# One decay matrix for both scan directions: the time step moves into the exponent

## The chip, the cores and the metric

The kernel runs on one core of a Trainium2 chip. The metric is device time in microseconds (us) of one execution. The engines that matter here are TensorE (PE, matrix products), VectorE (DVE, elementwise work), ScalarE (ACT, activation functions and copies), GpSimd (POOL) and SyncE (SP, which issues the weight loads). Each engine works through its own list of instructions in order and waits on semaphores for the others.

## What is computed

The reference is one inference step of a two-layer trunk (D = 1024) over 384 tokens: 256 latent tokens and 128 context tokens. Each layer has one input projection, three token mixers beside each other (pooling, differential attention, and a bidirectional state-space scan called SSD), gates, branch and output projections, and a gated feed-forward block. The change touches the SSD scan alone:

```
xdt = x * dt
y_diag = einsum(cc, bc, exp(segsum(dt * a)), xdt)        # inside a chunk of 128 tokens
y_off  = einsum(cc, h_enter, exp(cumsum(dt * a)))        # from the state that enters the chunk
...
y = y_forward + flip(y_backward) + D * x                 # both directions, summed
```

There are 8 heads of 64 channels, in 2 groups of 4 heads that share the matrices B and C, and 3 chunks of 128 tokens (two latent, one context). For one head and one chunk, the inner part of a direction is a 128x128 matrix, decay(s, t) * dt(s) * (B C)(s, t), times the 128x64 block of x. The forward matrix is zero on one side of the diagonal, the backward one on the other; the diagonal belongs to both.

## The kernel before

One core computes everything, channels on the 128 partitions and the 384 tokens in the free dimension. Weights stream from memory in *units* of 128x1024 elements, and the order of the units (UNITS) is the order of all the work: per layer 8 units for the scan's inputs, then u, q, k, v, then 4 units z, 24 gate units, 12 branch units, 8 output units and the feed-forward block. For each unit SP loads it, ACT copies its high part (`hi`, L1155), DVE subtracts to get the low part (`lo`, L1508), and PE does three products for each of 8 blocks (`three`, L823 to L825: 128x128 weights on 384 columns). Three units of high and low parts are held at once, so ACT and DVE prepare unit u+3 while PE is at unit u.

The three token mixers have no weights of their own to stream. They are laid by hand into *slots*: slot s runs beside unit MIX0+s, MIX0 being the first z unit. On PE the mixers' part of a slot stands after the unit's products (function `mixers`). On DVE it stands in two parts around the preparation of the next weights (`mixers_a`, then `lo`, then `mixers_b`). Attention fills slots 0 to 14; the time steps dt are made in slots 1 to 3 (tiles dtv, dte, dtt, adt), and their running sums (tile sm) in slot 3. Then come the chunks' transposes (slots 14 to 16), the normalisation of the attention output (slots 15 to 19: rst, then ot) and the states between chunks (slots 16 to 20: xw, hst).

The scan itself is six tasks y_ = 0 to 5 (chunk c = y_ // 2, head group g = y_ % 2), one in every second slot from slot 19. A task goes round through three engines:

1. PE `rows` (L1053) spreads the running sums of 4 heads over 128 partitions, one bank for each direction.
2. DVE `decays` (L1782) adds to each head's 128x128 block a number per partition (tile nac, minus the running sum) and a mask of 0 and -1e30: 8 instructions, into tile ee, [direction][head x 128].
3. ACT exponentiates ee in place (L1397, 128x1024), and for the latent chunks also the banks into eb (L1396).
4. DVE `matrices` (L1793, L1797) multiplies each head's block of ee by dt (tile dtt, a number per partition) and by the group's B C matrix (tile bg): 8 instructions of 128x128. For the latent chunks it also multiplies eb by C, 128x512 for each direction. The last one raises m_done.
5. PE `scan_out` (L1075) waits for m_done and multiplies, two slots after `rows`: for each head two products of xt with ee (one for each direction) and, for the latent chunks, two of the entering states hst with eb, all into one 64x128 output. Even heads write partitions 0 to 63 and odd heads 64 to 127.
6. DVE `gate_z` (L1810, L1814) adds D x and multiplies by z. Then the next task's `decays` follows on DVE.

After the last task come the grouped normalisation (L1115, L1116, L1908), the split of its result into high and low parts, and the branch units of the scan.

`chunk_weights` (L1864, slot 7) also makes nac. `step.then(...)` raises a semaphore and makes the same engine wait for it, so that the next instruction may read the result.

Of the kernel before, what the change touches and what calls it, by code (L numbers as in the profile page):

```python
# [26 lines left out]
ALU = mybir.AluOpType  # L27
ACT = mybir.ActivationFunctionType
AX = mybir.AxisListType

P = 128
# [9 lines left out]
CHUNK0 = (0, P, CTX0)  # L41
NCH = 3
# [3 lines left out]
SSD_H, SSD_P, SSD_G = 8, 64, 2  # L46
# [4 lines left out]
FFN = ((8 * D // 3 + 127) // 128) * 128  # L51
FT = FFN // P
NEG = -1e30


XBC, UU, QQ, KK, VV, ZZ, GATE, BRANCH, OUT, UP, DOWN = (
# [165 lines left out]
def count(l, per, i):  # L222

    return l * per + i + 1
# [60 lines left out]
def build(nc, wstream, whead, par, bias, tab, xs, xp, cvec, cvec_rows, kc, vc, st0, fng, y, newk, newv, news):  # L285
    ctx = ExitStack()
    with ctx:
# [3 lines left out]
        def sem(name):  # L291
            return ctx.enter_context(nc.semaphore(name))
# [10 lines left out]
        with ExitStack() as a:  # L303
            gates = sb("gates", [P, 24, T], where=a)
            xbc = sb("xbc", [P, 8, T], where=a)
# [27 lines left out]
        with ExitStack() as a:  # L333
            xt = sb("xt", [P, NCH, 4 * P], where=a)
            bg = sb("bg", [P, NCH, 4 * P], where=a)
# [4 lines left out]
            ee = sb("ee", [P, 2, 4 * P], where=a)  # L340
            eb = sb("eb", [P, 2, 4 * P], where=a)
# [42 lines left out]
        dte = sb("dte", [P, 48])  # L384
        dtt = sb("dtt", [P, 48])
# [3 lines left out]
        sm = sb("sm", [P, 144])  # L389
# [97 lines left out]
        dt_in = sem("dt_in")  # L487
        dt_raw = sem("dt_raw")
        dt_log = sem("dt_log")
        adt_done = sem("adt_done")  # L490
        ada_done = sem("ada_done")
        bd_done = sem("bd_done")
# [270 lines left out]
        def _(pe):  # L763
# [293 lines left out]
            def scan_out(l, y_):  # L1057
                c, g = divmod(y_, 2)
                pe.wait_ge(m_done, count(l, NY, y_))
                if y_:  # L1060
                    pe.wait_ge(yz_done, count(l, NY, y_ - 1))
                else:
                    pe.wait_ge(st_done, count(l, 4, 3))
                    pe.wait_ge(state_in, 32 * (l + 1))
                for i in range(4):
                    h = 4 * g + i
                    out = mix7[64 * (i % 2):64 * (i % 2) + 64, P * (i // 2):P * (i // 2) + P]
                    hs = slice(SSD_P * h, SSD_P * h + SSD_P)
                    ms = slice(P * i, P * i + P)
                    terms = [(xt[:, c, hs], ee[:, d, ms]) for d in range(2)]  # L1070
                    if c < 2:

                        terms += [(hst[:, (0, 3)[d] if c == 0 else (2, 1)[d], hs], eb[:, d, ms]) for d in range(2)]
                    for n, (s_, m_) in enumerate(terms):
                        last = mm(out, s_, m_, start=(n == 0), stop=(n == len(terms) - 1))  # L1075
                last.then_inc(y_done, 1)
# [66 lines left out]
        def _(act):  # L1143
# [184 lines left out]
            def mixers(l, s):  # L1328
# [40 lines left out]
                if SLOT_A <= s < SLOT_A + HEADS:  # L1369
                    h = s - SLOT_A  # L1370
                    if h == HEADS - 1:
                        act.preload_act_table_set(LN_EXP)
                    act.wait_ge(misc_done, count(l, NMISC, M_ATT + h))
                    af(rst[:, h, :], mz, ACT.Copy).then_inc(att_ss, 1)
                    if h == HEADS - 1:
                        act.wait_ge(att_ss, count(l, HEADS, h))
                        step.then(af(rst[:, :, :], rst[:, :, :], ACT.Ln, bias=eps, scale=1.0 / P))
                        af(rst[:, :, :], rst[:, :, :], ACT.Exp, scale=-0.5).then_inc(ors_done, 1)
# [119 lines left out]
        def _(dve):  # L1498
# [287 lines left out]
            def matrices(l, y_):  # L1786
                c, g = divmod(y_, 2)
                dve.wait_ge(e_done, count(l, NY, y_))
                for d in range(2):
                    for i in range(4):  # L1790
                        col = 16 * c + SSD_H * d + 4 * g + i
                        m_ = ee[:, d, P * i:P * i + P]
                        last = stt(out=m_, in0=m_, scalar=dtt[:, col:col + 1], in1=bg[:, c, P * (2 + g):P * (3 + g)],  # L1793
                                   op0=ALU.mult, op1=ALU.mult)
                    if c < 2:
                        e3 = eb[:, d, :].rearrange("p (i t) -> p i t", i=4)
                        last = tt(e3, e3, xbc[:, 6 + g, CHUNK0[c]:CHUNK0[c] + P].unsqueeze(1).to_broadcast([P, 4, P]),  # L1797
                                  ALU.mult)
                last.then_inc(m_done, 1)

            def gate_z(l, y_):
# [16 lines left out]
            def mixers_a(l, s):  # L1818
                if s < NATT:
                    softmax_max(l, s)  # L1820
                if s == 1:
                    dve.wait_ge(misc_done, count(l, NMISC, M_DTT))
                    step.then(tt(dtv[:, :].rearrange("p (c h) -> p c h", c=NCH),
                                 mz[:, 0:48].rearrange("p (c h) -> p c h", c=NCH),
                                 prm_("dtb", 0, 16).unsqueeze(1).to_broadcast([P, NCH, 16]), ALU.add))
                    stt(out=dte[:, :], in0=dtv[:, :], scalar=-1.0, in1=dtv[:, :], op0=ALU.mult, op1=ALU.min) \
                        .then_inc(dt_raw, 1)
                if s == 3:
                    dve.wait_ge(misc_done, count(l, NMISC, M_SM))
                    nc.vector.tensor_copy(sm[:, :], mz[:, 0:144])  # L1830
                    step.then(nc.vector.tensor_copy(csh_[0:96, :], mz[0:96, 2 * P:3 * P]))
                    tt(csl[0:96, :], mz[0:96, 2 * P:3 * P], csh_[0:96, :].bitcast(F32), ALU.subtract).then_inc(sm_done, 1)
                if SLOT_PW <= s < SLOT_PW + 4:
                    j = s - SLOT_PW
                    dve.wait_ge(misc_done, count(l, NMISC, M_PW + j))
                    ts(ut[:, j, 0:T], mz, prm_("pscale", j), None, ALU.mult).then_inc(op_done, 1)
                if s == SLOT_SPLIT:
                    for i in range(4):
                        low(l, SP_OP + i, hl[:, i, :], ut[:, i, 0:T], hh[:, i, :])
                if scan_task(s, Y_SLOTS) is not None:  # L1840
                    gate_z(l, scan_task(s, Y_SLOTS))
                if SLOT_S <= s < SLOT_S + 2:
                    enter_state(l, s - SLOT_S)
                if SLOT_S - 1 <= s < SLOT_S + 3:
                    weighted(l, s - SLOT_S + 1)
                if s == SLOT_A + HEADS:
                    dve.wait_ge(ors_done, l + 1)
                    for h in range(HEADS):
                        last = stt(out=ot[:, h, :], in0=ot[:, h, :], scalar=sg[:, 0:1], in1=rst[:, h, :], op0=ALU.mult,
                                   op1=ALU.mult)  # L1850
                    last.then_inc(on_done, 1)
                if scan_task(s) is not None:
                    decays(l, scan_task(s))

            def block_diagonal(l, i):

                if i == 0:
# [3 lines left out]
                stt(out=bd[0:96, i, :], in0=csh_[0:96, :].bitcast(F32), scalar=heads[0:96, i:i + 1],  # L1861
                    in1=bd[0:96, i, :].bitcast(F32), op0=ALU.mult, op1=ALU.add).then_inc(bd_done, 1)

            def chunk_weights(l):  # L1864

                ts(nac[:, :], sm[:, 0:48], -1.0, None, ALU.mult)
                dve.wait_ge(ede_done, l + 1)
                for d in range(2):
                    last = tt(wdc[:, 24 * d:24 * d + 24].rearrange("p (c h) -> p c h", c=NCH),
                              dtt[:, :].rearrange("p (c h) -> p c h", c=NCH)[:, :, SSD_H * d:SSD_H * d + SSD_H],  # L1870
                              ede[:, 24 * d:24 * d + 24].rearrange("p (c h) -> p c h", c=NCH), ALU.mult)
                last.then_inc(wdc_done, 1)

            def mixers_b(l, s):
# [5 lines left out]
                if s == 2:  # L1880

                    dve.wait_ge(dt_log, l + 1)
                    step.then(stt(out=dtt[:, :], in0=dtv[:, :], scalar=0.0, in1=dte[:, :], op0=ALU.max, op1=ALU.add))
                    stt(out=adt[:, :].rearrange("p (c h) -> p c h", c=NCH), in0=dtt[:, :].rearrange("p (c h) -> p c h", c=NCH),
                        scalar=-1.0, in1=eal[:, :].unsqueeze(1).to_broadcast([P, NCH, 16]), op0=ALU.mult,
                        op1=ALU.mult).then_inc(adt_done, 1)

                    step.then(nc.vector.memset(ada[:, :, :, :], 0.0))
                    dve.wait_ge(adt_done, l + 1)
                    a3 = adt[:, :].rearrange("p (c h) -> p c h", c=NCH)  # L1890
                    for d in range(2):
                        for n in range(2):
                            at = 16 * n + SSD_H * d
                            last = nc.vector.tensor_copy(ada[:, :, d, at:at + SSD_H], a3[:, :, SSD_H * d:SSD_H * d + SSD_H])
                    last.then_inc(ada_done, 1)
# [235 lines left out]
```

## Time and profile before

| | |
|---|---|
| median of 3 runs | 1383.5 us (1382.97 to 1384.87) |
| profiled execution | 1383.34 us |
| its span, first to last instruction | 1381.6 us |
| PE busy | 1313.4 us (95%) |
| DVE busy | 1093.5 us (79%) |
| ACT busy | 646.8 us (47%) |
| POOL busy | 162.6 us (12%) |
| mean granted TensorE clock | 0.991 of full speed |

Busy times of PE overlap, since a product starts before the one ahead of it has drained; what a product costs in a row of products is the distance from start to start. The same holds, in a small way, for DVE. The six scan tasks of layer 0 lie between 268 and 340 us, those of layer 1 between 941 and 1013 us.

### The profile page before, as it was taken

Reading aid. Unit: us, or ns where it says so; the run is one execution under the profiler, and the core shown is the slowest. Engines: PE = TensorE matmul, PEld = TensorE weight load, DVE = VectorE, ACT = ScalarE, POOL = GpSimd, SP = SyncE. Lnnn points to the kernel's source line nnn. Section 1 sums busy time; section 2 is a strip of 40 time slices with the busy share of each in tenths; the row PEclk is TensorE's granted clock in tenths of the full one; section 3 lists DMA queues with packets and bytes.
Section 4 is the critical chain, followed back from the end, with each engine's and each line's share of the span. In section 5 each row is a group of like instructions: output and inputs, shape, how many; then the busy total and the mean of one; then the engine's idle time right before and its main releaser. Section 6 shows DMA issues by size and latency. Waiting matters only on the chain.

```text
span 1381.6 us, 20127 instructions
## 1 busy us (share of the span) xinstructions
PE 1313.4 (95%) x7564; PEld 1243.7 (90%) x7564; DVE 1093.5 (79%) x2102; ACT 646.8 (47%) x1035; POOL 162.6 (12%) x166
## 2 busy tenths in 40 slices
PE   5899999999999999999989999999999899999996
PEld 4799889999988999999979988898999799999996
DVE  5889988679857999999967998637877699989432
ACT  4643445644556444442355335445445654454331
POOL 0058000000210000000100930000031000000001
PEclk8999999999999999999999999999999999999998
DMA  9456535323343454447734572333224244454431
GB/s 361 142 203 209 195 107 198 139 96 104 111 147 100 160 168 152 153 160 258 258 134 153 206 249 79 107 107 107 84 101 152 89 155 143 147 168 132 140 126 46
DMA packets 58289, 208.95 MB, mean 151 GB/s; under 512 B 6736, under 2 KB 8912, under 8 KB 56784
## 3 DMA queue, kind: packets, MB, share of 16 engines
q1 hardware_dynamic: 55648, 197.53, 42.7%
q0 software_dynamic: 2544, 10.13, 2.2%
q8 instruction: 60, 0.98, 0.3%
q14 instruction: 37, 0.30, 0.1%
HBM read 203.97 MB, written 3.67 MB: 150 GB/s over the span
## 4 chain that ended last, share of the span: by engine, by line
PE 44%; DVE 37%; issue 8%; ACT 8%; DMA 1%; POOL 0%; SPq 0%; DVEq 0%; ACTq 0%; POOLq 0%
PE acc L823 12%; PE acc L825 12%; PE acc L824 12%; DVE wl L1508 8%; DVE cv L1658 6%; DVE junk_front L1583 5%; DVE junk_ffn L1583 5%; ACT wh L1155 1%; DVE gates L1702 1%; DVE cv L1679 1%; PE mix L1075 1%; DVE al L1513 1%; ACT ah L1172 1%; DVE x L1720 1%; PE mix L980 1%
## 5 line engine op out<-in xcount | busy, mean ns | idle before, releaser
L823 PE MATMUL acc<-hh,wh 128*128 128x384 f32 x1528 | 524.1, 343 | 14.3 <-DVE wl L1508 11.6
L825 PE MATMUL acc<-hh,wl 128*128 128x384 f32 x1528 | 511.3, 335 | 0.0
L824 PE MATMUL acc<-hl,wh 128*128 128x384 f32 x1528 | 511.1, 334 | 0.0
L1508 DVE TENSOR_TENSOR wl<-raw,wh 128x1024 fp32r<-128x1024 f32 (+1 forms) x280 | 344.8, 1233 | 126.1 <-ACT wh L1155 124.4
L1155 ACT ACTIVATE wh<-raw 128x1024 fp32r<-128x1024 f32 (+1 forms) x280 | 290.7, 1041 | 111.2 <-PE acc L825 110.2
L823 PEld LDWEIGHTS acc<-hh,wh 128*128 128x128 f32 x1528 | 286.8, 188 | 35.0 <-DVE wl L1508 20.9
L824 PEld LDWEIGHTS acc<-hl,wh 128*128 128x128 f32 x1528 | 287.0, 188 | 2.4
L825 PEld LDWEIGHTS acc<-hh,wl 128*128 128x128 f32 x1528 | 286.8, 188 | 0.0
L1658 DVE SCALAR_TENSOR_TENSOR cv<-acc,prm,cv 128x1 f32<-128x1 f32 (+1 forms) x416 | 153.7, 412 | 11.3 <-ACT cv L1276 4.2
L823 PE MATMUL acc<-ah,wh 128*128 128x384 f32 x352 | 119.1, 338 | 3.1 <-DVE wl L1508 2.7
L824 PE MATMUL acc<-al,wh 128*128 128x384 f32 x352 | 118.3, 336 | 0.0
L825 PE MATMUL acc<-ah,wl 128*128 128x384 f32 x352 | 118.2, 336 | 0.0
L1583 DVE SCALAR_TENSOR_TENSOR junk_ffn<-rawm,crow 128x1024 f32<-128x1024 f32 x80 | 99.0, 1275 | 0.0
L1172 ACT ACTIVATE ah<-cv 128x384 fp32r<-128x384 f32 x44 | 23.2, 527 | 139.6 <-DVE cv L1679 139.6
L1583 DVE SCALAR_TENSOR_TENSOR junk_front<-rawm,crow 128x1024 f32<-128x1024 f32 x64 | 87.4, 1401 | 0.0
L823 PEld LDWEIGHTS acc<-ah,wh 128*128 128x128 f32 x352 | 66.5, 189 | 5.4 <-DVE wl L1508 5.4
L1276 ACT ACTIVATE cv<-acc,prm 128x384 f32<-128x384 f32 x104 | 68.6, 659 | 5.6 <-PE acc L825 5.6
L1302 ACT ACTIVATE gates<-acc,bgh 128x384 f32<-128x384 f32 x48 | 28.0, 582 | 83.3 <-PE acc L825 83.3
L825 PEld LDWEIGHTS acc<-ah,wl 128*128 128x128 f32 x352 | 66.6, 189 | 0.0
L824 PEld LDWEIGHTS acc<-al,wh 128*128 128x128 f32 x352 | 66.6, 189 | 0.0
L1314 ACT ACTIVATE th<-cv 128x384 f32<-128x384 f32 x60 | 31.6, 527 | 71.5 <-DVE cv L1658 71.5
L1258 ACT ACTIVATE th<-x 128x384 f32<-128x384 f32 x28 | 14.8, 528 | 81.8 <-DVE x L1720 81.8
(256 smaller groups left out, 1673.1 us busy)
## 6 DMA issues: line engine op xcount, KB each, us to landing
raw<-in_wstream_dram SPq DMA_DIRECT2D x248, 512.0 KB, 3.5
rawm<-in_wstream_dram SPq DMA_DIRECT2D x80, 512.0 KB, 3.8
raw<-in_wstream_dram SPq DMA_DIRECT2D x32, 448.0 KB, 3.3
head<-in_whead_dram SPq DMA_DIRECT2D x8, 1024.0 KB, 14.0
crow<-in_cvec_rows_dram POOLq DMA_DIRECT2D x2, 1024.0 KB, 5.2
out_y_dram<-gates POOLq DMA_DIRECT2D x8, 192.0 KB, 2.7
prm<-in_par_dram POOLq DMA_DIRECT2D x2, 591.5 KB, 4.3
x<-in_xs_dram SPq DMA_DIRECT2D x1, 1024.0 KB, 8.9
```

The source lines that it names most:

```text
L823: mm(out, sh, mhi, start=start, stop=False)
L824: mm(out, sh, mlo, start=False, stop=False)
L825: return mm(out, sl, mhi, start=False, stop=stop)
L1155: af(wh[:, s, 0:n], raw[:, raw_slot(u), 0:n], ACT.Copy).then_inc(hi_done, 1)
L1172: af(dst, src, ACT.Copy).then_inc(h_hi, 1)
L1258: af(th[:, j % 2, :], x[:, j, :], ACT.Square).then_inc(sq_done, 1)
L1276: af(cv[:, b_, :], bank[:, 0:T], ACT.Identity, bias=prm_(b, tile), scale=prm_(w, 3 * tile + 1)) \
L1302: af(gates[:, j, :], bank[:, 0:T], ACT.Tanh, bias=bgh[:, j:j + 1], scale=0.5).then_inc(g_done, 1)
L1314: af(th[:, b_, :], cv[:, b_, :], ACT.Tanh).then_inc(cv_tanh, 1)
L1508: tt(wl[:, s, 0:n], raw[:, raw_slot(u), 0:n], wh[:, s, 0:n].bitcast(F32), ALU.subtract).then_inc(lo_done, 1)
L1583: last = stt(out=junk[:, v, :], in0=rawm[:, n % NMOD, :], scalar=1.0, in1=rows[:, v, :], op0=ALU.mult, op1=ALU.mult, accum_out=macc[:, m, ...
L1658: return stt(out=out, in0=src, scalar=prm_(w, 3 * tile + i), in1=out, op0=ALU.mult, op1=ALU.add)
```

## The change

The time step dt(s) is a factor of a whole partition s in both directions' matrices. After the change it stands in the exponent as ln dt. In slot 2 DVE writes dt, floored at 1e-37, to dte; in slot 18 ACT takes its logarithm in place (semaphores dt_floor and ln_done); in slot 19 DVE makes nac = ln dt - running sum, in two instructions (new function `exponents`), in place of the one in slot 7. The exponentials then hold dt. `matrices` adds the two directions' blocks of ee into one (128x512), waits for that, and multiplies the sum by the B C matrix once (128x512, the matrix repeated over the 4 heads). `scan_out` has one product with ee for each head in place of two. The products with eb stay.

```diff
--- before.py
+++ after.py
@@ -51,6 +51,7 @@
 FFN = ((8 * D // 3 + 127) // 128) * 128
 FT = FFN // P
 NEG = -1e30
+TINY = 1e-37
 
 
 XBC, UU, QQ, KK, VV, ZZ, GATE, BRANCH, OUT, UP, DOWN = (
@@ -487,6 +488,8 @@
         dt_in = sem("dt_in")
         dt_raw = sem("dt_raw")
         dt_log = sem("dt_log")
+        dt_floor = sem("dt_floor")
+        ln_done = sem("ln_done")
         adt_done = sem("adt_done")
         ada_done = sem("ada_done")
         bd_done = sem("bd_done")
@@ -1067,7 +1070,7 @@
                     out = mix7[64 * (i % 2):64 * (i % 2) + 64, P * (i // 2):P * (i // 2) + P]
                     hs = slice(SSD_P * h, SSD_P * h + SSD_P)
                     ms = slice(P * i, P * i + P)
-                    terms = [(xt[:, c, hs], ee[:, d, ms]) for d in range(2)]
+                    terms = [(xt[:, c, hs], ee[:, 0, ms])]
                     if c < 2:
 
                         terms += [(hst[:, (0, 3)[d] if c == 0 else (2, 1)[d], hs], eb[:, d, ms]) for d in range(2)]
@@ -1370,6 +1373,8 @@
                     h = s - SLOT_A
                     if h == HEADS - 1:
                         act.preload_act_table_set(LN_EXP)
+                        act.wait_ge(dt_floor, l + 1)
+                        af(dte[:, :], dte[:, :], ACT.Ln).then_inc(ln_done, 1)
                     act.wait_ge(misc_done, count(l, NMISC, M_ATT + h))
                     af(rst[:, h, :], mz, ACT.Copy).then_inc(att_ss, 1)
                     if h == HEADS - 1:
@@ -1786,16 +1791,13 @@
             def matrices(l, y_):
                 c, g = divmod(y_, 2)
                 dve.wait_ge(e_done, count(l, NY, y_))
-                for d in range(2):
-                    for i in range(4):
-                        col = 16 * c + SSD_H * d + 4 * g + i
-                        m_ = ee[:, d, P * i:P * i + P]
-                        last = stt(out=m_, in0=m_, scalar=dtt[:, col:col + 1], in1=bg[:, c, P * (2 + g):P * (3 + g)],
-                                   op0=ALU.mult, op1=ALU.mult)
-                    if c < 2:
-                        e3 = eb[:, d, :].rearrange("p (i t) -> p i t", i=4)
-                        last = tt(e3, e3, xbc[:, 6 + g, CHUNK0[c]:CHUNK0[c] + P].unsqueeze(1).to_broadcast([P, 4, P]),
-                                  ALU.mult)
+                step.then(tt(ee[:, 0, :], ee[:, 0, :], ee[:, 1, :], ALU.add))
+                m3 = ee[:, 0, :].rearrange("p (i t) -> p i t", i=4)
+                last = tt(m3, m3, bg[:, c, P * (2 + g):P * (3 + g)].unsqueeze(1).to_broadcast([P, 4, P]), ALU.mult)
+                for d in range(2 if c < 2 else 0):
+                    e3 = eb[:, d, :].rearrange("p (i t) -> p i t", i=4)
+                    last = tt(e3, e3, xbc[:, 6 + g, CHUNK0[c]:CHUNK0[c] + P].unsqueeze(1).to_broadcast([P, 4, P]),
+                              ALU.mult)
                 last.then_inc(m_done, 1)
 
             def gate_z(l, y_):
@@ -1844,6 +1846,7 @@
                 if SLOT_S - 1 <= s < SLOT_S + 3:
                     weighted(l, s - SLOT_S + 1)
                 if s == SLOT_A + HEADS:
+                    exponents(l)
                     dve.wait_ge(ors_done, l + 1)
                     for h in range(HEADS):
                         last = stt(out=ot[:, h, :], in0=ot[:, h, :], scalar=sg[:, 0:1], in1=rst[:, h, :], op0=ALU.mult,
@@ -1861,9 +1864,17 @@
                 stt(out=bd[0:96, i, :], in0=csh_[0:96, :].bitcast(F32), scalar=heads[0:96, i:i + 1],
                     in1=bd[0:96, i, :].bitcast(F32), op0=ALU.mult, op1=ALU.add).then_inc(bd_done, 1)
 
+            def exponents(l):
+
+                dve.wait_ge(ln_done, l + 1)
+                for d in range(2):
+                    last = tt(nac[:, 24 * d:24 * d + 24].rearrange("p (c h) -> p c h", c=NCH),
+                              dte[:, :].rearrange("p (c h) -> p c h", c=NCH)[:, :, SSD_H * d:SSD_H * d + SSD_H],
+                              sm[:, 24 * d:24 * d + 24].rearrange("p (c h) -> p c h", c=NCH), ALU.subtract)
+                step.then(last)
+
             def chunk_weights(l):
 
-                ts(nac[:, :], sm[:, 0:48], -1.0, None, ALU.mult)
                 dve.wait_ge(ede_done, l + 1)
                 for d in range(2):
                     last = tt(wdc[:, 24 * d:24 * d + 24].rearrange("p (c h) -> p c h", c=NCH),
@@ -1881,6 +1892,7 @@
 
                     dve.wait_ge(dt_log, l + 1)
                     step.then(stt(out=dtt[:, :], in0=dtv[:, :], scalar=0.0, in1=dte[:, :], op0=ALU.max, op1=ALU.add))
+                    ts(dte[:, :], dtt[:, :], TINY, None, ALU.max).then_inc(dt_floor, 1)
                     stt(out=adt[:, :].rearrange("p (c h) -> p c h", c=NCH), in0=dtt[:, :].rearrange("p (c h) -> p c h", c=NCH),
                         scalar=-1.0, in1=eal[:, :].unsqueeze(1).to_broadcast([P, NCH, 16]), op0=ALU.mult,
                         op1=ALU.mult).then_inc(adt_done, 1)
```

## Rows read from the trace of the kernel before

**Rows 1.** The page, part 4: the chain that ended last, by engine.

```profile
PE 44%; DVE 37%; issue 8%; ACT 8%; DMA 1%; POOL 0%; SPq 0%; DVEq 0%; ACTq 0%; POOLq 0%
```

**Rows 2.** The chain in time, layer 0: start us, length us, engine, tile, line.

```profile
268.11 0.69 DVE xw L1757
...
278.80 2.57 PE mix L1075 x32
...
290.53 2.50 PE mix L1075 x32
...
313.75 0.19 PE acc L825
...
315.94 1.97 DVE hl L1513 x4
...
341.85 0.88 PE misc L1115 x2
...
379.20 0.44 PE acc L823
```

**Rows 3.** The same chain in layer 1.

```profile
951.78 2.57 PE mix L1075 x32
...
1052.21 0.44 PE acc L823
```

**Rows 4.** DVE in order of time, layer 0: start, length, what, [idle before].

```profile
205.79 0.26 DVE L1869 TENSOR_TENSOR wdc<-dtt,ede 128x24 f32<-128x24 f32 x2
...
263.02 0.69 DVE L1766 TENSOR_TENSOR hst<-hst,ede 128x512 f32<-128x512 f32 x1 [2.52 <-PE mix L1037]
263.75 0.69 DVE L1769 TENSOR_TENSOR hst<-hst,mix 128x512 f32<-128x512 f32 x1
...
275.35 1.14 DVE L1793 SCALAR_TENSOR_TENSOR ee<-ee,dtt,bg 128x128 f32<-128x128 f32 x4 [1.03 <-ACT ee L1397]
276.40 0.68 DVE L1797 TENSOR_TENSOR eb<-eb,xbc 128x512 f32<-128x512 f32 x1
277.01 1.13 DVE L1793 SCALAR_TENSOR_TENSOR ee<-ee,dtt,bg 128x128 f32<-128x128 f32 x4
...
322.33 2.19 DVE L1793 SCALAR_TENSOR_TENSOR ee<-ee,dtt,bg 128x128 f32<-128x128 f32 x8
324.44 1.01 DVE L1702 SCALAR_TENSOR_TENSOR gates<-gates,acc 128x384 f32<-128x384 f32 x2
```

**Rows 5.** PE in order of time, layer 0, around two of the scan's products.

```profile
277.71 0.34 PE L825 MATMUL acc<-hh,wl 128*128 128x384 f32 x1
278.80 0.65 PE L1075 MATMUL mix<-ee,xt 128*64 128x128 f32 x4 [0.74 <-DVE eb L1797]
279.28 0.27 PE L1075 MATMUL mix<-eb,hst 128*64 128x128 f32 x1
279.29 0.32 PE L1075 MATMUL mix<-ee,xt 128*64 128x128 f32 x1
279.39 0.27 PE L1075 MATMUL mix<-eb,hst 128*64 128x128 f32 x1
...
281.29 0.72 PE L1053 MATMUL mix<-bd,selr 32*128 32x512 f32 x2
...
325.29 0.34 PE L825 MATMUL acc<-hh,wl 128*128 128x384 f32 x1
325.56 1.14 PE L1075 MATMUL mix<-ee,xt 128*64 128x128 f32 x16
326.63 0.72 PE L1053 MATMUL mix<-bd,selr 32*128 32x512 f32 x2
```

**Rows 6.** ACT in order of time, layer 0, slots 2 and 18.

```profile
170.53 0.24 ACT L1352 ACTIVATE dte<-dte 128x48 f32<-128x48 f32 x1
...
264.35 0.49 ACT L1374 ACTIVATE rst<-misc 128x384 f32<-128x384 f32 x1
...
266.49 1.49 ACT L1378 ACTIVATE rst<-rst 128x1536 f32<-128x1536 f32 x1
```

## The prediction

> **What bounds the kernel now.** I read the chain of work that ended last first. By engine it is shared between PE and DVE, with little of ACT and hardly any DMA [rows 1], so the question for each stage is which of the two is the late one. In order of time it shows three stretches around the scan [rows 2]. From 268.11 to 278.80 it runs on DVE: the last state weights, then the attention normalisation, `decays`, the exponentials and `matrices` of task 0. From 278.80 to 313.75 it is on PE: four `scan_out` of the latent chunks (2.50 to 2.57 us each, two of them shown) and the weight units between them. From 315.94 to 341.85 it is on DVE again, through `decays` and `matrices` of tasks 4 and 5. After that the normalisation and the scan's branch units follow, on DVE most of the time, until PE takes over at 379.20. Layer 1 repeats all this 672.98 us later: 278.80 answers to 951.78, and 379.20 to 1052.21 within 0.03 us [rows 3]. So both engines are worth something, each in its own stretch, and I work out one layer and double it.
>
> The lists of DVE and PE in order of time give the prices. A latent `scan_out` takes 281.29 - 278.80 = 2.49 us for 16 products, one of the context chunk 326.63 - 325.56 = 1.07 us for 8 [rows 5]. Each product is two records here (16 records for the 8 products of the context task). In the first one the records of ee and eb mix at 279.28, 279.29 and 279.39: even and odd heads write different halves of the partitions, and these rows show that the next head's ee runs beside this head's eb.
>
> **The change part by part.**
>
> *`matrices` on DVE.* Four of the old 128x128 instructions take 276.40 - 275.35 = 1.05 us from start to start, so the eight of a latent task take 2.10; the eight of a context task take 324.44 - 322.33 = 2.11 [rows 4]. The new pair is an addition with a wait behind it and a multiplication. A 128x512 instruction that the next one has to wait for costs 263.75 - 263.02 = 0.73, one without such a wait 277.01 - 276.40 = 0.61 [rows 4]; together 1.34. Each task gains 2.10 - 1.34 = 0.76, or 0.77 in the context chunk. Behind the new wait stand only the multiplication, the eb instructions and the next weights.
>
> *`scan_out` on PE.* Four products of 16, or of 8, go. In proportion that is 2.49 / 4 = 0.62 for a latent task and 1.07 / 2 = 0.53 for a context task. The bounds of the first are wide, since the trace has no head with three products. A product alone on its half costs 0.24, from the four records between 278.80 and 279.28 [rows 5]. If what remains of eb (two products, 0.49 a head) never overlaps from head to head, the new time is 0.24 + 4 x 0.49 = 2.2 and the gain 0.29; if each removed product gives back all its 0.24, the gain is 0.96. I take 0.62, since rows of both kinds of task show work on two halves at once.
>
> The Trainium skill, "TensorE: Matmul & The Clock Gate", Part 3, says that matmuls start and end strictly in program order, whatever half of the array they use. In the order of the source the next head's ee stands behind all eb of this head, so by that rule the four products of a head would run one after another and nothing of an ee would be hidden, which is the bound of 0.96. The trace does not agree: the ee record at 279.29 starts before the eb record at 279.39 [rows 5].
>
> *The logarithm on ACT, slot 18.* One 128x48 instruction costs 0.24 [rows 6]. It stands between the table load and the copy at 264.35, for which the right table is already there. It makes the normalisation's last instruction end at 266.49 + 1.49 + 0.24 = 268.22 instead of 267.98. DVE asks for that result only when it is through with xw, at 268.80 [rows 2], so it is hidden; without that cover it would cost 0.24. The wait for dt_floor, with that copy and the normalisation queued behind it, is met some 90 us earlier (slot 2 is near 171).
>
> *`exponents` on DVE, slot 19.* Two 128x24 instructions take 0.26 [rows 4], and the wait behind them 0.04 (0.73 less the 0.69 of the instruction [rows 4]), so 0.30. They come behind xw at 268.11, on the path, and push the normalisation of ot and `decays` of task 0. Their own wait, for the logarithm, ends near 264.6, 4 us before. The dropped instruction of slot 7 and the added one of slot 2 are one small 128x48 instruction each, both in the attention slots, where DVE has the same to do as before; I put them at 0 with 0.1 either way.
>
> *What the path does with it, layer 0.* PE goes from its last unit product to `scan_out` in 325.56 - 325.29 = 0.27 when nothing holds it; before task 0 it takes 278.80 - 277.71 = 1.09, so it waits 0.82 there [rows 5]. `matrices` now ends 0.76 - 0.30 = 0.46 earlier, all of it inside that wait: gain 0.46, and 0.36 of waiting is left. For tasks 1 to 3 PE is the late engine and DVE's 0.76 buys nothing. What counts there is the shorter `scan_out` of tasks 0, 1 and 2 ahead of the last gate unit: 3 x 0.62 = 1.86. The last gate unit's end releases the high parts and then DVE at 315.94 [rows 2], so DVE enters its stretch 2.32 earlier. `scan_out` of task 3 and those of tasks 4 and 5 lie beside it and give PE room but not the path. On DVE two context `matrices` follow: 2 x 0.77 = 1.54. What is late next is still DVE: PE would reach 341.85 with 0.46 + 4 x 0.62 + 2 x 0.53 = 4.0 in hand, DVE with 2.32 + 1.54 = 3.86. From there to 379.20 everything hangs on that chain, and what follows on PE starts as much earlier.
>
> Sum: 3.86 a layer, 7.7 for two. From the profiled execution's own 1383.34 that is 1375.6; the median of the runs, 1383.5, stands 0.2 above it, which I leave out. The measurement of this kernel can tell about 0.2%, 2.8 us, from no change.
>
> **The rivals.**
>
> *Smaller: eb holds the halves apart.* If the remaining eb products do not overlap, a latent `scan_out` gains 0.29 only: 0.46 + 0.87 + 1.54 = 2.9 a layer, 5.7 in all, 1377.6. For it: in the rows it is always an ee that runs beside an eb. Against: in the context task two ee run beside each other, so the halves themselves are free to. If `exponents` also cost twice what I take, 0.6 goes, and the time is 1378.2.
>
> *Larger: each removed product is worth all its 0.24.* Then 0.46 + 3 x 0.96 + 1.54 = 4.9 a layer, 9.8 in all, 1373.6. PE would then keep 5.4 in hand and DVE sets the end. Against it: 16 products at 0.24 would be 3.8, and 2.49 were measured.
>
> *Slower: the heads fall out of step.* With one ee and two eb in a head the mixing of the halves could break, and each of the 12 products would take its lone 0.24: 2.9, which is 0.4 more than now. PE would then lose 4 x 0.4 = 1.6 and gain 0.46 and about 0.2 from the context tasks (4 x 0.24 = 0.96 against 1.07), so it comes to 341.85 some 0.9 late: 1.8 in all at most, 1385.2. It decides once a latent `scan_out` grows by more than (0.46 + 0.2) / 4 = 0.17. To be slower by 0.2%, 1.4 a layer, it would have to grow by 0.5, to 3.0. Against it: less work in the same order has no row that shows more time.
>
> *Nothing: the time given back is taken later.* The chain is unbroken to 379.20 and PE is on it afterwards, so I see no place for this. It would need weights that come late, and DMA holds 1% of the chain [rows 1].
>
> **How the numbers follow.** Forecast 0.58; smaller 0.22; larger 0.12; slower or nothing 0.08, of which within 0.2% either way 0.06 and beyond it 0.02. Predicted time 1375.6. The forecast's own spread is 1374.5 to 1376.8 (0.1 either way in each of the small instructions and in each `scan_out`). The range reaches to the larger rival and past the smaller one: 1373.3 to 1379.0. All cases but the last are faster by more than 0.2%: faster 0.92, same 0.06, slower 0.02.
>
> **What would show it.** In the changed profile: the ee instructions of `matrices` as 128x512, with about 1.34 from the start of the addition to the start of the next instruction; a latent `scan_out` of 24 records near 1.87, a context one of 8 near 0.54; the wait of PE before task 0's `scan_out` down to about 0.36 and none before tasks 1 to 3; the two small instructions of `exponents` between xw and ot, with no idle time; no further table load on ACT; the chain still on PE in the latent tasks and on DVE in the context tasks, and PE taking over 3.9 us earlier than 379.20. The prediction is wrong if a latent `scan_out` stays near 2.49 or goes below 1.6, if DVE waits for the logarithm, or if the branch units begin earlier but end no earlier.

## The result, and the profile after

The changed kernel takes 1376.39 us (median of 4 runs, 1374.89 to 1377.44), the kernel before, in turn with it, 1384.18 (1382.97 to 1384.9): a ratio of 0.9944 [0.9927, 0.9961], 7.8 us less. The forecast was 1375.6. The execution that was profiled is the slowest of the four: 1377.44, with a span of 1375.7 and a mean granted clock of 0.987.

DVE in order of time, changed kernel, layer 0 (columns and counterparts in [rows 4]):

```profile
267.55 0.69 DVE L1762 TENSOR_TENSOR xw<-xt,wdc 128x512 f32<-128x512 f32 x1 [1.94 <-PE mix L1040]
268.16 0.27 DVE L1871 TENSOR_TENSOR nac<-dte,sm 128x24 f32<-128x24 f32 x2
268.46 2.21 DVE L1852 SCALAR_TENSOR_TENSOR ot<-ot,sg,rst 128x384 f32<-128x384 f32 x4
...
275.09 0.69 DVE L1794 TENSOR_TENSOR ee<-ee 128x512 f32<-128x512 f32 x1 [1.03 <-ACT ee L1402]
275.82 0.69 DVE L1796 TENSOR_TENSOR ee<-ee,bg 128x512 f32<-128x512 f32 x1
276.43 1.28 DVE L1799 TENSOR_TENSOR eb<-eb,xbc 128x512 f32<-128x512 f32 x2
```

The addition and the multiplication of `matrices` take 276.43 - 275.09 = 1.34 us, as the prediction had it. The two instructions of `exponents` stand between xw and ot: 268.46 - 268.16 = 0.30, with no idle time ahead of them. Xw starts 0.56 earlier than in [rows 2]. Of the change only three small instructions, added or dropped (slots 2, 7 and 18), stand ahead of it, and the lead is there before the first of them: a weight copy of ACT starts at 99.35 in place of 99.93, and slot 2 is near 171. So this 0.56 is a difference between two executions, and I take it off below.

ACT in order of time, changed kernel, slot 18 (counterparts in [rows 6]), and its first copy of results in the feed-forward block:

```profile
262.49 1.28 ACT L1375 ACT_TABLE_LOAD   x1
263.78 0.24 ACT L1377 ACTIVATE dte<-dte 128x48 f32<-128x48 f32 x1
...
266.06 1.48 ACT L1383 ACTIVATE rst<-rst 128x1536 f32<-128x1536 f32 x1
...
424.57 0.66 ACT L1279 ACTIVATE cv<-acc,prm 128x384 f32<-128x384 f32 x1
```

The logarithm takes 0.24 behind the table load that was there already, and the normalisation ends at 267.54, before DVE is through with `exponents` at 268.46.

PE in order of time, changed kernel, around task 0, a context task, and the start of the feed-forward block (counterparts of the first two in [rows 5]):

```profile
277.15 0.34 PE L828 MATMUL acc<-hh,wl 128*128 128x384 f32 x1
277.77 0.43 PE L1078 MATMUL mix<-ee,xt 128*64 128x128 f32 x2 [0.28 <-DVE eb L1799]
278.04 0.27 PE L1078 MATMUL mix<-eb,hst 128*64 128x128 f32 x1
278.05 0.32 PE L1078 MATMUL mix<-ee,xt 128*64 128x128 f32 x1
278.15 0.27 PE L1078 MATMUL mix<-eb,hst 128*64 128x128 f32 x1
...
279.50 0.72 PE L1056 MATMUL mix<-bd,selr 32*128 32x512 f32 x2
...
321.81 0.66 PE L1078 MATMUL mix<-ee,xt 128*64 128x128 f32 x8
322.40 0.72 PE L1056 MATMUL mix<-bd,selr 32*128 32x512 f32 x2
...
411.29 0.63 PE L922 MATMUL acc<-hh,wh 128*128 128x384 f32 x1 [2.74 <-ACT hh L1224]
```

A latent `scan_out` takes 279.50 - 277.77 = 1.73, a context one 322.40 - 321.81 = 0.59. Before task 0 PE goes from unit product to `scan_out` in 0.62, so 0.35 of the wait is left.

The chain of work that ended last, changed kernel, both layers (counterparts in [rows 2, 3]):

```profile
277.77 1.80 PE mix L1078 x24
...
299.68 1.73 PE mix L1078 x24
...
312.59 1.97 DVE hl L1518 x4
...
374.27 0.44 PE acc L826
...
948.74 1.80 PE mix L1078 x24
...
1045.25 0.44 PE acc L826
```

The chain has the same shape as before: on PE through the latent tasks, on DVE through the context tasks, until PE takes over. What came of it in layer 0: 315.94 - 312.59 = 3.35 less the 0.56 of the start, 2.79, at DVE's entry, and 379.20 - 374.27 = 4.93 less 0.56, **4.37 us**, where PE takes over. In layer 1 xw starts 941.10 - 938.51 = 2.59 ahead and PE takes over 1052.21 - 1045.25 = 6.96 ahead, again 4.37. So the scan gives 8.7 us in two layers, 1.0 more than the 7.7 predicted. From profile to profile the end comes only 5.9 earlier. The lead shows where the rest went: 4.93 at 379, 2.59 at 941, 6.96 at 1052, 5.9 at the end. So 2.34 were given back between the scans, and 1.06 behind the second.

Most of that is the clock. Stretches of 8 us around the start of the feed-forward block, the two layers, changed kernel (stretch, length, then busy time and count of PE, PEld, DVE, ACT, POOL, the granted TensorE clock, DMA share, GB/s):

```profile
407.00:415.00 8.00, 5.26 (x16) 4.21 (x17) 6.75 (x14) 6.47 (x14) 0.00 (x0) 0.79 0.36 125
1080.00:1088.00 8.00, 5.76 (x24) 5.79 (x25) 6.61 (x15) 7.22 (x17) 0.00 (x0) 0.79 0.21 66
```

The kernel before, 5 and 8 us later. That is the same work in the first layer; in the second the stretch begins 1 us further into it:

```profile
412.00:420.00 8.00, 5.25 (x26) 4.20 (x27) 6.76 (x14) 6.46 (x14) 0.00 (x0) 1.00 0.34 121
1088.00:1096.00 8.00, 6.77 (x39) 6.80 (x40) 6.88 (x16) 7.59 (x18) 0.00 (x0) 1.00 0.17 62
```

Kernel before, the first product behind the gap ahead of the feed-forward block, and ACT's first copy of results:

```profile
416.25 0.41 PE L919 MATMUL acc<-hh,wh 128*128 128x384 f32 x1 [2.75 <-ACT hh L1221]
...
428.49 0.66 ACT L1276 ACTIVATE cv<-acc,prm 128x384 f32<-128x384 f32 x1
```

The busy time of PE in the first stretch is the same to 0.01, but it holds 16 records in place of 26. PE stands idle for 2.74 us while ACT makes the input of the feed-forward block, and behind that gap part of the stretch runs at 1.2 GHz, half speed. The first product takes 0.63 us there. The kernel before has the same gap (2.75), until 416.25, and 0.41 for the product behind it. By that product the changed kernel is 416.25 - 411.29 = 4.96 ahead, by the first copy of results on ACT 428.49 - 424.57 = 3.92. So a drop costs 1.04 us here. In layer 1 the lead falls from 1089.23 - 1082.24 = 6.99 to 1101.45 - 1095.54 = 5.91 over the same steps, so by 1.08. Two drops are 2.1 of the 3.4 us given back.

The largest piece of the other 1.3, between the first drop and 941, is a wait of DVE for weights that come late in layer 1, changed kernel:

```profile
823.15 1.23 DVE L1588 SCALAR_TENSOR_TENSOR junk_front<-rawm,crow 128x1024 f32<-128x1024 f32 x1 [0.80 <-DMA rawm<-in_wstream_dram]
```

In the kernel before the same instruction starts at 825.71 with no wait. By ACT's instructions on both sides the lead is 798.34 - 794.91 = 3.43 ahead of it and 829.79 - 827.24 = 2.55 behind it. A wait of this kind is also in the second profile of the changed kernel (0.70, below) and in three of the other experiments (0.27 to 1.17), one of them a form of the kernel before; it is in none of the three kernels with filled gaps, two of which have the change. So the change alone does not bring it, and why these weights come late in some executions is not shown. Some 0.4 us are left, in smaller steps that the traces don't settle.

### The profile page after: what moved, and what is told of

It reads as the page before. It is cut to its first block, busy times and chain, and to the rows that moved or that the text cites. A ratio compares the mean times of both kernels' runs of the same rounds, so it can differ in the third digit from the quotient of the medians.

```text
span 1375.7 us, 19871 instructions
## 1 busy us (share of the span) xinstructions
PE 1308.8 (95%) x7468; PEld 1239.1 (90%) x7468; DVE 1084.6 (79%) x2034; ACT 645.6 (47%) x1037; POOL 162.8 (12%) x166
## 4 chain that ended last, share of the span: by engine, by line
PE 45%; DVE 36%; issue 8%; ACT 7%; DMA 2%; POOL 0%; SPq 0%; ACTq 0%; DVEq 0%; POOLq 0%
PE acc L826 12%; PE acc L828 12%; PE acc L827 12%; DVE wl L1513 7%; DVE cv L1663 6%; DVE junk_front L1588 5%; DVE junk_ffn L1588 5%; ACT wh L1158 1%; DVE gates L1707 1%; DVE cv L1684 1%; DVE al L1518 1%; ACT ah L1175 1%; PE mix L983 1%; DVE x L1725 1%; DVE ee L1787 1%
```

## The experiments

Two questions were open: what each part of the change gives by itself, and whether the clock explains that the totals say less than the scan.

### One part alone

Only the products fewer, in the kernel before:

```
-                    terms = [(xt[:, c, hs], ee[:, d, ms]) for d in range(2)]
+                    terms = [(xt[:, c, hs], ee[:, 0, ms])]
```

> The kernel before, with one product with ee per head on PE instead of two; DVE, ACT and nac as before. It leaves the backward direction out of the inner part of a chunk. My theory (the path is on PE in the latent tasks and on DVE in the context tasks): a latent scan_out takes 1.73 us as in the changed kernel, DVE enters its stretch (the high parts' split, 315.94 us before) 3 x 0.76 = 2.3 us earlier counted from the scan's start, nothing more is gained on DVE, PE takes over 2.3 us earlier in each layer: about 4.6 us in all, 3 to 6. Rival (PE is busy 95% of the span, so all its removed work counts): 4 x 0.76 + 2 x 0.45 = 3.9 us a layer, 8 us in all.

Measured: 1380.16 (1379.34 to 1381.15, 10 runs) beside 1384.96 for the kernel before (24 runs), ratio 0.9955 [0.994, 0.997], 4.8 us less. The chain of work in its layer 0:

```profile
277.49 1.80 PE mix L1075 x24
...
312.30 1.96 DVE hl L1513 x4
...
375.58 0.45 PE acc L823
```

Xw starts at 266.81 here, so PE takes over 375.58 - 266.81 = 108.77 after it, against 379.20 - 268.11 = 111.09 before: 2.32 a layer, which is 3 x (2.49 - 1.73) = 2.28 and 0.04. Products alone give the three latent tasks ahead of DVE's entry and nothing of the context tasks.

Only `matrices`, in the changed kernel, with four products again (the inner part counts twice):

```
-                    terms = [(xt[:, c, hs], ee[:, 0, ms])]
+                    terms = [(xt[:, c, hs], ee[:, 0, ms]) for d in range(2)]
```

> The changed kernel with two products with ee per head on PE again: the second repeats the first, so the inner part of a chunk counts twice. DVE and ACT as changed. My theory: DVE gains 0.46 us before task 0 and 0.77 in each of tasks 4 and 5, 2.0 us a layer, but PE, with all its old products, has only 0.46 of that plus the 0.4 us that it waited in the context tasks, and it ends last at the normalisation: 0.85 us a layer, 1.7 us in all. Rival A (the two parts of the change simply add): 2.0 us a layer, 4.0 in all. Rival B (DVE's work is hidden behind PE): 0 to 0.9 us in all.

Measured: 1380.86 (1379.25 to 1383.65, 10 runs), ratio 0.9962 [0.9946, 0.9978], 4.1 less. The chain of work in its layer 0:

```profile
276.34 2.57 PE mix L1078 x32
...
311.49 2.50 PE mix L1078 x32
...
323.19 1.07 PE mix L1078 x16
...
376.00 0.44 PE acc L826
```

Now the chain stays on PE through task 3 and the context tasks, where the kernel before has DVE [rows 2]. Xw starts at 266.12, so PE takes over 109.88 after it: 1.21 a layer, 2.4 for two; 1.7 of the 4.1 lies outside the scan. Alone the two parts give 2.32 + 1.21 = 3.53 a layer, together 4.37. With either part alone the other engine takes the lead, and what its partner gains is room.

### The order of the products

A latent `scan_out` at 1.73 is shorter than three quarters of 2.49. Two explanations were left: the time goes by how the records of the two halves lie in program order, or by a price for each record. The heads of a pair take turns here, in the changed kernel and in the kernel before:

```
-                for i in range(4):
+                def product(i):
...
+                for i in (0, 2):
+                    for both in zip(product(i), product(i + 1)):
+                        for out, s_, m_, first, end in both:
+                            last = mm(out, s_, m_, start=first, stop=end)
```

> The changed kernel with scan_out's products ordered by pairs of heads: a product of the even head, then one of the odd head, so that neighbours write different halves of the partitions. My theory (each half works by itself at 0.12 us a record, and PE looks only a few records ahead in program order): 12 records on each half at 0.12 give 1.45 to 1.55 us for a latent scan_out in place of 1.73; a context one stays near 0.6. Three of them lie on the path of each layer, so 0.6 us a layer, 1.2 us in all against the changed kernel. Rival (the cost is one of issue, 0.072 us a record whatever the half): 1.73 stays, no change.

> The kernel before with its 16 products in the same order by pairs of heads. My theory: 16 records on each half at 0.12, so 1.95 to 2.05 us in place of 2.49, three of them on the path of each layer: 1.5 us a layer, 3 in all. Then more than half of what the change takes from PE in a latent task was to be had by the order alone. Rival (issue): 2.49 stays, no change.

Measured, changed kernel in turn: 1375.37 (1374.36 to 1376.45, 5 runs), ratio 0.9934 [0.9922, 0.9947] to the kernel before (1385.06, 15 runs). PE in order of time:

```profile
277.11 0.44 PE L1081 MATMUL mix<-ee,xt 128*64 128x128 f32 x4 [0.28 <-DVE eb L1802]
277.38 0.61 PE L1081 MATMUL mix<-eb,hst 128*64 128x128 f32 x8
277.82 0.39 PE L1081 MATMUL mix<-ee,xt 128*64 128x128 f32 x4
278.04 0.61 PE L1081 MATMUL mix<-eb,hst 128*64 128x128 f32 x8
278.57 0.72 PE L1056 MATMUL mix<-bd,selr 32*128 32x512 f32 x2
```

Measured, kernel before in turn: 1381.41 (1378.87 to 1382.32, 11 runs), ratio 0.9973 [0.9963, 0.9983], 3.65 less. PE in order of time:

```profile
276.57 0.66 PE L1078 MATMUL mix<-ee,xt 128*64 128x128 f32 x8 [0.74 <-DVE eb L1800]
277.06 0.61 PE L1078 MATMUL mix<-eb,hst 128*64 128x128 f32 x8
...
278.47 0.72 PE L1053 MATMUL mix<-bd,selr 32*128 32x512 f32 x2
```

The same products, in another order, take 1.46 in place of 1.73 and 1.90 in place of 2.49. A price for each record would have left both as they were. With 24 records, 12 on each half, 1.46 / 12 = 0.122; with 32, 1.90 / 16 = 0.119: each half takes one record in 0.12 us, and the halves run beside each other when their records alternate in program order. By that step 1.73 is about 14 steps and 2.49 about 21, against 12 and 16 if the halves always ran beside each other and 24 and 32 if they never did. So in source order they overlap for part of the time only; the rows show it at the seams, where one head's last records meet the next head's first (278.05 beside 278.04 and 278.15 above, and [rows 5]).

The path follows: the kernel before in turn has PE take over 375.18 - 265.89 = 109.29 after xw, 1.80 a layer, for 3 x 0.59 = 1.77; the changed kernel in turn 372.81 - 266.89 = 105.92, 5.17 a layer, 0.80 more than the changed kernel, for 3 x 0.27 = 0.81. In the time of the whole the second does not show: 1375.37, against 1374.54 for the changed kernel on the same chip (below). Its profile has the granted clock at half from 410, 694 and 711 us, that of the changed kernel on that chip from 693 alone, and DVE waits 1.17 us for the late weights of layer 1 in place of 0.70.

### The clock

Products that nobody reads, in PE's gaps ahead of the input of a block; the same edit in the kernel before and in the changed kernel:

```
+                        if l or u:
+                            for _ in range(3):
+                                mm(mix5[:, :], ident, tb[:, TAB["le"][0]:TAB["le"][0] + 512], start=True, stop=True)
                         joint(l, u, SP_N2 if u else SP_N1)
```

> The kernel before, with three products of constants (128x512, fp32, nobody reads the result) on PE ahead of the joint start of the feed-forward block in both layers and of layer 1, where PE has nothing to do for 2.7 us. My theory on the 3 us that the changed profile gives back outside the scan: TensorE's granted clock falls to half behind these gaps in some executions and not in others. Then the granted clock stays at 1.00 behind the filled gaps, and the time is that of the kernel before less 0 to 2 us, with less spread. Rival (the clock has nothing to do with it): same time, or later by what the products overrun the gap, up to 1 us in all.

> The changed kernel with the same three products in the same three gaps. My theory: no half clock behind the gaps (the changed profile has 0.79 and 0.60 there), the 1.0 us lost at each comes back, so 1 to 3 us less than the changed kernel, and 8 to 9 us less than the kernel before with the same products (2 x 4.4 from the scan). Rival: the difference of the two filled kernels stays at 6 to 7 us, and what was given back is given back elsewhere.

Measured: before 1380.54 (1379.21 to 1381.49, 11 runs), ratio 0.9958 [0.9943, 0.9974]; changed 1373.77 (1372.52 to 1378.27, 6 runs), 0.9916 [0.989, 0.9942]. The kernel before gains 4.4 where 0 to 2 were expected, and its runs spread over 2.3 us in place of 10. The filled kernels differ by 6.8, within the 6 to 7 of the rival and short of the 8 to 9 of my theory. The stretches tell why that number does not decide for the rival. Changed kernel, filled:

```profile
405.00:413.00 8.00, 6.55 (x23) 4.07 (x24) 6.95 (x17) 5.79 (x12) 0.00 (x0) 1.00 0.39 131
690.00:700.00 10.00, 7.78 (x36) 7.46 (x35) 5.34 (x16) 5.80 (x10) 1.11 (x2) 0.83 0.63 210
```

Kernel before, filled:

```profile
690.00:700.00 10.00, 7.76 (x45) 7.44 (x44) 9.77 (x24) 3.66 (x7) 2.72 (x3) 1.00 0.59 189
```

Filling kept the clock at full speed behind the feed-forward gap, where the changed kernel had 0.79. But at the layer boundary the clock still fell in the changed kernel and not in the one before, whose lead over its unfilled profile grows by 1.57 us there. The gap behind which it fell is a fourth one, and the products don't fill it: PE waits there for DVE to split weights (wl), and the products of layer 1 stand 15 us later. Changed kernel, filled:

```profile
692.88 0.69 PE L826 MATMUL acc<-ah,wh 128*128 128x384 f32 x1 [2.22 <-DVE wl L1516]
...
708.37 2.74 PE L1139 MATMUL mix<-tb 128*128 128x512 f32 x6
```

So the two profiled executions should differ by the scan less this fall, 2 x 4.37 - 1.57 = 7.17, and they differ by 1380.81 - 1373.54 = 7.27. Over the ten profiles of this document, half clock begins around the end of this open gap, within 2 us of it, in eight. Of the other three gaps (2.74 us) it does so at 9 of 21 that are open and at none of the 9 that are filled. Runs of a filled kernel can still be late: 1378.27, at a mean granted clock of 0.988, is one of the six.

The changed kernel again, unedited, on the chip of the kernels in turn:

> The changed kernel once more, on the same chip as the others, for its spread. My theory: the scan gives 4.4 us a layer in every execution, and the granted clock falls to half behind one, two or three of the gaps, each worth 1 to 1.6 us, so the runs lie between 1374 and 1378. Rival (something in the change itself gives 2 to 3 us back in every execution): the runs agree within 1 us, with the clock at half behind the same gaps each time.

Measured: 1374.54 (1373.92 to 1377.47, 5 runs), ratio 0.9931 [0.9917, 0.9945]. Stretches of its profile, a run of 1374.54:

```profile
412.00:420.00 8.00, 8.00 (x49) 8.00 (x48) 5.42 (x12) 7.81 (x18) 0.00 (x0) 1.00 0.01 2
690.00:700.00 10.00, 7.79 (x37) 7.48 (x36) 5.59 (x17) 5.53 (x10) 1.35 (x2) 0.83 0.61 211
```

The same program with the same gap (PE idle for 2.74 us until 411.08), and here the clock stays at full speed behind it. Its scan takes 374.07 - 267.36 = 106.71 from xw, 4.38 a layer, as in the first profile. So the gain of the scan is firm, and the 1374 to 1377 of the whole follows for the most part how often the clock falls: its five runs take 1373.92 to 1374.82 at a mean granted clock of 0.989 to 0.991 and 1377.47 at 0.987, and the first four 1374.89 at 0.990, 1375.72 at 0.988, and 1377.07 and 1377.44 at 0.987.

### All of it together

The changed kernel with the heads in turn, the gaps filled, and `exponents` ahead of the last `weighted`, where DVE was idle:

```
+                if s == SLOT_A + HEADS:
+                    exponents(l)
                 if SLOT_S - 1 <= s < SLOT_S + 3:
                     weighted(l, s - SLOT_S + 1)
                 if s == SLOT_A + HEADS:
-                    exponents(l)
```

> The changed kernel with the products in turn, exponents moved ahead of the last state weights in slot 19 (where DVE waits 1.9 us for PE anyway), and the three products of constants in the three gaps of PE. My theory: 1.2 us from the order, 0.3 a layer from exponents (PE's wait before task 0's scan_out falls from 0.35 to about 0), and no half clock behind at least the two gaps ahead of the feed-forward block: 1371 to 1373, less than every kernel so far. Rival (issue, and DVE not late there): no less than the changed kernel with filled gaps, 1373.8.

Measured: 1369.38 (1369.08 to 1374.45, 5 runs), ratio 0.9899 [0.9884, 0.9915], the best of all and below what was expected. DVE in order of time:

```profile
264.81 0.27 DVE L1878 TENSOR_TENSOR nac<-dte,sm 128x24 f32<-128x24 f32 x2
266.86 0.69 DVE L1768 TENSOR_TENSOR xw<-xt,wdc 128x512 f32<-128x512 f32 x1 [1.78 <-PE mix L1040]
267.47 2.20 DVE L1859 SCALAR_TENSOR_TENSOR ot<-ot,sg,rst 128x384 f32<-128x384 f32 x4
```

A stretch at the layer boundary:

```profile
690.00:700.00 10.00, 8.81 (x51) 8.81 (x52) 5.02 (x7) 4.87 (x9) 0.00 (x0) 1.00 0.70 230
```

`exponents` now lies in the idle time ahead of xw, and ot follows xw at once. PE takes over at 372.42, 105.56 after xw: 5.53 a layer, 0.36 more than in turn alone, of which 0.30 is `exponents`. Its clock is at full speed from 42 to 1359 us, although the 2.2 us gap at the layer boundary is open here too, and DVE does not wait for late weights in layer 1. In the profile of the changed kernel on this chip a fall stands there and a wait of 0.70; I had not counted on the absence of either, and five runs don't tell whether it is luck. One run of the five, 1374.45, has a mean clock of 0.988 in place of 0.991 or 0.992.

## Why the prediction was right, point by point

- *`matrices`, `exponents`, the logarithm.* 1.34, 0.30 and a hidden 0.24, each as predicted. No table load was added.
- *The wait of PE before task 0.* 0.35 is left, 0.36 was predicted; there is none before tasks 1 to 3.
- *`scan_out`: the mis-sized term.* In proportion it was to gain 0.62 in a latent task; it gained 0.76 (a context task gained 0.48 for 0.53). Proportion was the wrong rule: a head's products go through one half in steps of 0.12, and only the seams between two heads overlap, so what counts is the length of the chain in program order, about 21 steps before and 14 after. How far past a head's end PE can overlap no run varies. The bounds (0.29 and 0.96) held it. "eb holds the halves apart" and "the heads fall out of step" both fell: with one ee and two eb in a head the mixing got better, not worse. The Trainium skill, "TensorE: Matmul & The Clock Gate", Part 3, has matmuls start and end strictly in program order; the trace of after does not agree either: the next head's ee starts at 278.05, ahead of this head's eb at 278.15. Order does matter, though: 1.73 against 1.46 for the same products.
- *The sum.* With the measured terms the prediction's own sum is 0.46 + 3 x 0.76 + 2 x 0.77 = 4.28 a layer; 4.37 was measured in both layers. The same sum gives 5.09 for the changed kernel in turn (5.17 measured). Which engine is late where was right too, and the parts alone confirm it, with one exception: for `matrices` alone I had expected 0.85 a layer, and 1.21 came. PE reaches the normalisation 0.95 earlier (338.91 - 266.12 = 72.79 after xw against 341.85 - 268.11 = 73.74), and the other 0.26 comes behind it, where I had counted nothing. One reading of the chain was wrong: between 278.80 and 313.75 it has three `scan_out` (at 278.80, 290.53 and 302.23), not four. The sum had three.
- *"What follows on PE starts as much earlier."* True of the start, not of the end. The 8.7 of the scan became 5.9 between the two profiles, since the clock fell behind the feed-forward gaps in the one and not in the other (2.1), and 1.3 more was lost between the scans, 0.8 of it to weights that came late. This is the step that the prediction did not have: its rival "the time given back is taken later" saw no place for it, though it named late weights as what it would need. That 7.8 us between the medians came so near to the 7.7 forecast is in part luck, since two errors met: 1.0 too little in the scan, and no price for the clock and the late weights. The 0.8 by which 1376.39 lies above 1375.6 is the distance of the median before, 1384.18, from the profiled 1383.34 that the forecast started from.

Not settled: some 0.4 us between the first scan's end and the second's start, why the weights of layer 1 come late in some executions, and what makes the clock fall behind the same gap in one execution and not in another.

## What to carry to other kernels

Two engines that set the end in turn must be shortened together: alone the two parts gave 2.32 and 1.21 us a layer, together 4.37. Where two small products write different halves of the partitions, put them in turn in program order; that by itself was worth 0.27 to 0.59 us of each `scan_out` and removed nothing. When a total says less than the stage that was changed, follow the lead over the kernel before along the trace, and look where it shrinks: here at the granted clock first, then at a wait for a transfer.

## What the runs showed of the hardware

- A half of the output partitions takes a record of these products (128 columns, float32, two records to a product) every 0.12 us, and the two halves run beside each other if their records alternate: 1.46 us for 12 products and 1.90 for 16, against 1.73 and 2.49 with the heads one after another.
- A gap of 2.74 us on PE was followed by half the granted clock in one execution of the changed kernel and not in another of the same program; over the ten profiles 9 of 21 such gaps were, 8 of 10 gaps of 2.2 us at the layer boundary, and none of 9 that were filled. A drop cost 1.04 and 1.08 us at the feed-forward block; at the layer boundary the kernel without it gained 1.57. Products that nobody reads, put into the gaps, brought the kernel before from 1384.96 to 1380.54 us.
